# Fewer, wider VectorE operations, squares and row copies on ScalarE, and new tables of places in a hybrid decoder step

## The reference, cut to what matters

```python
for i in range(2):
    mp, ms = modulation(c_prompt, ...), modulation(c_sample, ...)   # six rows of 1024 each
    h = rms_norm(y, norm1_g) * (1 + scale) + shift
    o = mla(h) if i == 0 else sgu_mixer(h)      # attention with a paged cache; gated MLP
    y = y + gate * o
    y = y + gate2 * peer(rms_norm(y, norm2_g) * (1 + scale2) + shift2)

def peer(x):                                    # per token
    q = x @ w_q                                 # 8 heads, two halves of 128
    t1, i1 = top_k(q1 @ keys0.T, 16); t2, i2 = top_k(q2 @ keys1.T, 16)
    top, ci = top_k(t1[:, None] + t2[None, :], 16)          # of 256 candidates
    idx = i1[ci // 16] * 128 + i2[ci % 16]      # 16 of 16384 experts
    act = gelu(dot(u_tab[idx], x))
    return sum(softmax(top) * act * v_tab[idx])
```

## Time and profile before

| | |
|---|---|
| times of three runs | 2204.23, 2215.53, 2223.11 us, median 2215.53 |
| the profiled execution | span 2207.0 us; its own time isn't labelled among the three |
| busy | PE 69%, DVE 63% (1395.3 us), POOL 55%, ACT 16% |
| moved | 751.57 MB, mean 341 GB/s |
| instructions | DVE 3469, ACT 901 |

### The profile page before, as it was taken

The page is one execution under the profiler, slowest core; times in us unless marked ns, Lnnn a source line. Parts: engine busy times, 40 slices in busy tenths (PEclk is TensorE's granted clock), DMA queues, the critical chain, the costliest instruction groups (busy, mean ns, idle before and its releaser), DMA issues. The chain is left out here.

```text
span 2207.0 us, 25764 instructions
## 1 busy us (share of the span) xinstructions
PE 1531.2 (69%) x9198; PEld 745.6 (34%) x9198; DVE 1395.3 (63%) x3469; ACT 355.5 (16%) x901; POOL 1212.1 (55%) x1097
## 2 busy tenths in 40 slices
PE   5676446865546879977687889968778850555567
PEld 2345113541123426533532437525423310111112
DVE  1447988599875655558498836499687327443641
ACT  0100112111112211013131201122223110111111
POOL 0004377545777574437475754467675438745774
PEclk8687778987877979888796888977887785578658
DMA  9719899998989899898798998989998889999998
GB/s 366 276 47 403 291 374 335 413 362 329 384 323 370 297 417 419 341 364 315 274 347 316 315 362 345 377 324 338 363 339 302 323 317 338 380 419 419 335 350 310
DMA packets 213942, 751.57 MB, mean 341 GB/s; under 512 B 27236, under 2 KB 35628, under 8 KB 213816
## 3 DMA queue, kind: packets, MB, share of 16 engines
q0 software_dynamic: 155136, 564.20, 68.4%
q1 hardware_dynamic: 58680, 185.72, 21.6%
HBM read 747.74 MB, written 2.10 MB: 340 GB/s over the span
## 5 line engine op out<-in xcount | busy, mean ns | idle before, releaser
L779 POOL DMA_INDIRECT uring<-in_peer_u,expert x512 | 580.6, 1134 | 511.5 <-DVE dots L1932 211.0
L1217 PE MATMUL yacc<-vring,diag 64*64 64x512 f32 x4096 | 653.6, 738 | 229.9 <-DMA vring<-in_peer_v,expert 163.2
L779 POOL DMA_INDIRECT vring<-in_peer_v,expert x512 | 556.4, 1087 | 425.8 <-PE yacc L1217 290.4
L1932 DVE CUSTOM_DVE_ANT_0 uring<-uring,h 128x1024 f32<-128x1024 f32 x512 | 615.3, 1225 | 161.4 <-DMA uring<-in_peer_u,expert 144.1
L1217 PEld LDWEIGHTS yacc<-vring,diag 64*64 64x64 f32 x4096 | 155.2, 156 | 610.0 <-DMA vring<-in_peer_v,expert 338.8
L1453 ACT ACTIVATE diag<-cst,wts 128x64 f32<-128x64 f32 (+1 forms) x528 | 172.9, 344 | 868.7 <-PE yacc L1217 630.0
L1005 PE MATMUL pp<-hT,wring 128*128 128x128 f32 x992 | 132.3, 294 | 21.7 <-issue 15.9
L1005 PEld LDWEIGHTS pp<-hT,wring 128*128 128x128 f32 x992 | 125.8, 208 | 35.4 <-issue 29.6
L1805 DVE TENSOR_REDUCE arena<-arena 128x16 f32<-128x1024 f32 x64 | 77.8, 1215 | 28.6 <-ACT arena L1392 27.7
L1706 DVE MAX8 t<-sc 128x8 f32<-128x128 f32 (+1 forms) x68 | 19.9, 292 | 117.5 <-ACT sc L1253 83.2
L1068 PE MATMUL pq<-w_uk,arena 128*128 128x512 f32 x128 | 74.6, 672 | 22.9 <-ACT arena L1392 22.9
(11 more groups left out here) (301 smaller groups left out, 1854.0 us busy)
## 6 DMA issues: line engine op xcount, KB each, us to landing
wring<-in_peer_w_q SPq DMA_DIRECT2D x47, 1024.0 KB
wring<-in_w_mod SPq DMA_DIRECT2D x38, 1024.0 KB
wring<-in_sg_w_in SPq DMA_DIRECT2D x48, 768.0 KB
wring<-in_sg_w_out SPq DMA_DIRECT2D x18, 1024.0 KB
wring<-in_mla_w_o SPq DMA_DIRECT2D x9, 1024.0 KB
uring<-in_peer_u,expert POOLq DMA_INDIRECT x512
vring<-in_peer_v,expert POOLq DMA_INDIRECT x512
uring<-in_w_mod SPq DMA_DIRECT2D x6, 1024.0 KB, 16.7
```

Of the source, the lines that this page charges most:

```text
L779: pool.indirect_dma_start(ring[:, slot % RING, :], None, table[n // 3], bass.IndirectOffsetOnAxis(ap=idx, axis=0)).then_inc(land[slot % RI ...
L1217: last = pe.matmul(yacc[64 * q:64 * q + 64, r], diag[at, slot % RING, :], v[at, 512 * q:512 * q + 512], start=first, stop=final)
L1932: dve.tensor_tensor_reduce(u, u, rows_h[:, :], 1.0, 0.0, ALU.mult, ALU.add, dots[:, p % 2, i:i + 1]).then_inc(u_used, 1)
```

## The change

- `rsqrt`: two fused instructions per step in place of four. `polynomial`: two in place of three.
- `pick`: the two sides together, on 512 columns, and one cast of 64 columns for both index pairs. The buffers `cu` and `ti` become one, and `cand` becomes a part of `hot`.
- `norm` of A and B: the sum of squares is an ACT `Square` with an accumulated output into `scr`.
- `gate_row` (in `proj`, `sgu_out` and `peer_out`) and `drain` move to ACT. The label lists follow.
- All five tables are new, with the same units (the sum of squares, the rows and the other stage instructions are places too). In POOL's string the eight K and C stand elsewhere by a few slots: the fourth C, for one, behind 244 U and 212 V before, and behind 249 U and 215 V after. In SP's, one chunk is loaded ahead of `x_prompt`, and 15 chunks ahead of `load_once` where there were 8.

The diff, with the tables' entries left out:

```diff
--- before.py
+++ after.py
@@ -109,67 +109,74 @@
 
 
 PLAN_PE = """
...
 """
 PLAN_ACT = """
...
 """
 PLAN_DVE = """
...
 """
 PLAN_POOL = """
...
 """
 PLAN_SP = """
...
 """
 
 
@@ -282,7 +289,7 @@
         if tile == S:
             rep = ["rep"] if step[3] else []
             return ["ssq", "hT0", "hT1"] + rep, ["sq", "h"], ["hT0", "hT1"] + rep
-        return ["rows", "hT0", "hT1"], ["h"], ["hT0", "hT1"]
+        return ["rows", "hT0", "hT1"], ["h"], ["sq", "hT0", "hT1"]
     if kind == "mla_in":
         return ["z", "cT", "qk"], ["c", "kr", "qk"], ["z", "cT", "qk", "sq"]
     if kind == "attn":
@@ -307,7 +314,7 @@
     if kind == "cache_out":
         return ["oT"], ["oT"], []
     if kind == "proj":
-        return ["row"] * (tile != S) + ["w0", "w1", "w2", "w3"], ["row"] * (tile != S) + ["x"], []
+        return ["row"] * (tile != S) + ["w0", "w1", "w2", "w3"], ["x"], ["row"] * (tile != S)
     if kind == "query":
         return [f"w{i}" for i in range(step[3])] + ["s"], [], ["q", "s"]
     if kind == "route":
@@ -331,9 +338,9 @@
     if kind == "sgu_s_mix":
         return ["ssq", "gT"], ["poly", "sq", "v", "gated", "gT"], ["tanh"]
     if kind == "sgu_out":
-        return ["row"] * (tile != S) + [f"w{i}" for i in range(6)], ["row"] * (tile != S) + ["x"], []
+        return ["row"] * (tile != S) + [f"w{i}" for i in range(6)], ["x"], ["row"] * (tile != S)
     if kind == "peer_out":
-        return ([], ["x"], []) if tile % 3 == S else (["y"], ["x"], [])
+        return ([], ["x"], []) if tile % 3 == S else (["y"], ["x"], ["row"])
     return [], [], []
 
 
@@ -443,9 +450,11 @@
         mrows, mbg = sb("mrows", [P, 12, 256]), sb("mbg", [P, 2, 256])
         scr, rs = sb("scr", [P, 64]), sb("rs", [P, 48])
         sc, work = sb("sc", [P, 4, 2, NKEYS]), sb("work", [P, 256])
-        t1, ti = sb("t1", [P, 2, TOPK]), sb("ti", [P, 2, TOPK], U32)
-        cand, hot = sb("cand", [P, TOPK * TOPK]), sb("hot", [P, TOPK, TOPK])
-        ctop, ci, cu = sb("ctop", [P, TOPK]), sb("ci", [P, TOPK], U32), sb("cu", [P, 2, TOPK], U32)
+        t1, picks = sb("t1", [P, 2, TOPK]), sb("picks", [P, 4, TOPK], U32)
+        cu, ti = picks[:, 0:2, :], picks[:, 2:4, :]
+        hot = sb("hot", [P, 2, TOPK, TOPK])
+        cand = hot[:, 0].rearrange("p a b -> p (a b)")
+        ctop, ci = sb("ctop", [P, TOPK]), sb("ci", [P, TOPK], U32)
         cf, ef = sb("cf", [P, 4, TOPK]), sb("ef", [P, 2, TOPK])
         eg = sb("eg", [P, TOPK + 4])
         kv, kr = sb("kv", [P, 16, KVR]), sb("kr", [P, 2, 16, ROPE])
@@ -586,6 +595,10 @@
         def mod_bank(row):
 
             return yacc[:, row % 2] if row < rows_before(FIRST_QUERY) else pq[:, 1]
+
+        def last_slot(n):
+
+            return SLOT0[max(p for p, s in enumerate(STEPS) if s[0] == n) + 1]
 
         points_seen = {}
 
@@ -1259,6 +1272,10 @@
             def norm(k, tile, layer, second):
                 point(k, 0)
                 begin(act, k)
+                if tile != S:
+                    if k == WHERE[("norm", A, 0, 0)]:
+                        act.wait_ge(in_x, 16)
+                    signal(act.activation(h_tok[tile][:, :], x[tile][:, :], ACT.Square, accum_out=scr[:, 0:1]), "sq")
                 for q in range(2):
                     after(act, PE, k, f"hT{q}")
                     if tile == S:
@@ -1310,6 +1327,23 @@
                         after(act, PE, k, f"pT{f}{q}")
                         signal(copy(att[:, 512 * q:512 * q + 512], ps[q][:, :]), f"pT{f}{q}")
 
+            def gate_row(k, tile, name):
+
+                after(act, PE, k, name)
+                signal(copy(h_tok[tile][:, :], pss[:, :, :].rearrange("p q n -> p (q n)")), "row")
+
+            def projection(k, tile):
+                begin(act, k)
+                if tile != S:
+                    gate_row(k, tile, "row")
+                for j in range(n_points(k) - 1):
+                    point(k, j)
+
+            def peer_out(k, n):
+                if n % 3 != S:
+                    begin(act, k)
+                    gate_row(k, n % 3, "y")
+
             def query(k, n, h, g):
                 begin(act, k)
                 for i in range(g - 1):
@@ -1458,7 +1492,13 @@
                 act.wait_ge(poly_ready, p + 1)
                 act.activation(ew[:, 2, 0:SLOTS[p]], ew[:, 0, 0:SLOTS[p]], ACT.Tanh, scale=GELU_K).then_inc(tanh_ready, 1)
 
-            spot = Spots(PLAN_ACT, D=diagonal, T=tanh)
+            def drain(i):
+
+                n = DRAINED[i]
+                act.wait_ge(v_used, last_slot(n))
+                copy(h_tok[n % 3][:, :], yacc[:, :, :].rearrange("p q n -> p (q n)")).then_inc(drained, 1)
+
+            spot = Spots(PLAN_ACT, D=diagonal, T=tanh, Y=drain)
 
             def point(k, j):
                 early(k, j, ACTE, lambda *a: None)
@@ -1466,7 +1506,7 @@
 
             stages = dict(init=init, norm=norm, mla_in=mla_in, attn=attn, query=query, route=route, query_s=query_s, topk_s=topk_s,
                           cache=cache, sgu_v=sgu_v, sgu_vnorm=sgu_vnorm, sgu_u=sgu_u, sgu_mix=sgu_vnorm,
-                          sgu_s=sgu_s, sgu_s_mix=sgu_s_mix)
+                          sgu_s=sgu_s, sgu_s_mix=sgu_s_mix, proj=projection, sgu_out=projection, peer_out=peer_out)
             for k, s in enumerate(SCHEDULE):
                 signals.start(k)
                 spot()
@@ -1477,7 +1517,7 @@
                         point(k, j)
                 point(k, n_points(k) - 1)
                 signals.end()
-            assert spot.done == dict(D=N_SLOTS, T=len(STEPS))
+            assert spot.done == dict(D=N_SLOTS, T=len(STEPS), Y=len(DRAINED))
 
 
         @block.vector
@@ -1516,9 +1556,8 @@
                 link(ts(out.bitcast(U32), out.bitcast(U32), -1.0, RSQRT_MAGIC, ALU.mult, ALU.add))
                 for _ in range(3):
                     link(tt(tmp, out, out, ALU.mult))
-                    link(tt(tmp, tmp, v, ALU.mult))
-                    link(ts(tmp, tmp, -0.5, 1.5, ALU.mult, ALU.add))
-                    link(tt(out, out, tmp, ALU.mult))
+                    link(stt(tmp, tmp, -0.5, v, ALU.mult, ALU.mult))
+                    link(stt(out, tmp, 1.5, out, ALU.add, ALU.mult))
 
             def square_sum(out, a, waste):
                 link(dve.tensor_tensor_reduce(waste, a, a, 1.0, 0.0, ALU.mult, ALU.add, out))
@@ -1564,7 +1603,7 @@
                 if tile == S:
                     quad_square_sum(k, xr, h)
                 else:
-                    square_sum(scr[:, 0:1], xr, h)
+                    after(dve, ACTE, k, "sq")
                 link(ts(scr[:, 0:1], ps[0][:, 0:1] if tile == S else scr[:, 0:1], 1.0 / D, EPS, ALU.mult, ALU.add))
                 rsqrt(scr[:, 1:2], scr[:, 0:1], rs[:, 0:1])
                 if tile != S:
@@ -1666,20 +1705,12 @@
                 if tile == S:
                     link(tt(h, acc[:, 0, 0:QUAD], sample_rows(mod_row(k))[0], ALU.mult))
                 else:
-                    if SCHEDULE[k][0] == "peer_out":
-                        link(cp(h, flat(pss)))
+                    after(dve, ACTE, k, "row")
                     link(tt(h, h, flat(acc), ALU.mult))
                 signal(tt(x[tile][:, :], x[tile][:, :], h, ALU.add), "x")
 
-            def gate_row(k, tile):
-
-                if tile != S:
-                    after(dve, PE, k, "row")
-                    signal(cp(h_tok[tile][:, :], flat(pss)), "row")
-
             def proj(k, tile):
                 begin(dve, k)
-                gate_row(k, tile)
                 for i in range(4):
                     point(k, i)
                 after(dve, PE, k, "w3")
@@ -1720,13 +1750,12 @@
                 point(k, mid)
                 link(ts(cu[0:r, 0, :], ci[0:r, :], 4, None, ALU.logical_shift_right))
                 link(ts(cu[0:r, 1, :], ci[0:r, :], 15, None, ALU.bitwise_and))
-                link(cp(cf[0:r, 0:2, :], cu[0:r, :, :]))
-                link(cp(cf[0:r, 2:4, :], ti[0:r, :, :]))
-                for i in range(2):
-                    hr = hot[0:r, :, :]
-                    link(tt(hr, over(cf[0:r, i, :], TOPK), times(const("iota16", r), TOPK), ALU.is_equal))
-                    link(tt(hr, hr, times(cf[0:r, 2 + i, :], TOPK), ALU.mult))
-                    link(dve.tensor_reduce(ef[0:r, i, :], hr, X, ALU.add))
+                link(cp(cf[0:r, :, :], picks[0:r, :, :]))
+                hr, h3 = hot[0:r, :, :, :], hot[0:r, :, :, :].rearrange("p i a b -> p (i a) b")
+                link(tt(h3, over(cf[0:r, 0:2, :].rearrange("p i a -> p (i a)"), TOPK), times(const("iota16", r), 2 * TOPK),
+                        ALU.is_equal))
+                link(tt(hr, hr, cf[0:r, 2:4, :].unsqueeze(2).to_broadcast([r, 2, TOPK, TOPK]), ALU.mult))
+                link(dve.tensor_reduce(ef[0:r, :, :].rearrange("p i a -> p (i a)"), h3, X, ALU.add))
                 link(stt(expert_out, ef[0:r, 0, :], float(NKEYS), ef[0:r, 1, :], ALU.mult, ALU.add))
                 after(dve, ACTE, k, "exp")
```

(18 more changed lines are left out.)

113 lines of the change are left out of this document (60 added, 53 removed).

## The result

The changed kernel takes 2240.5 us, median of five runs (2237.4 to 2266.2), against 2212.7 for the kernel before on the same chip. The ratio is 1.0157, with a 95% interval of 1.0103 to 1.0212: slower by one to two per cent, where I forecast 2183 and a range up to 2228. The profiled execution is the slowest of the five (span 2264.4). A second set of runs on another chip gave 1.0218 (1.0156 to 1.0279); its profiled execution is the fastest of its five (span 2223.2).

The account below looks back on a forecast made before the run. The prediction took DMA transfer to bound the kernel, with idle stretches to win back. From 2215.5 us, 4 + 22 + 10 gained and 4 given made 2183.5, say 2183 us, with a range of 2140 to 2228.

Parts of the forecast that it names:

- the DVE-bound stretches: Windows of 10 us with DVE busy 9 or more, transfer partly idle: shorter DVE work was to gain 22 us there.
- my two terms: Gains from less DVE work: 4 us in the serial chain at the start, 22 us where DVE is full.
- the 46 windows: Windows of 10 us with DVE busy 9 or more and DMA share below 0.97, holding 80.6 us of idle transfer.
- DVE's total: Work taken off DVE by picks, roots, polynomials, squares and row copies: about 104 us of its 1395.
- two readings: Gain where DVE is full: 32 us by its share of DVE work, 16 us by POOL's waits for dots; 22 taken.
- the third kind of idleness: Idle transfer where DVE is not full, but PE is or a table's order holds an engine back: 84 us.
- I take -10: New tables: the fourth C later in POOL's table frees eight gathers of 1.24 us from its wait, 10 us gained.
- the bound of +42: Worst case for the new tables: half as much again added to the 84 us of idle transfer where DVE is not full.
- the tables are the larger part: Rival, chance 0.15: a new order also takes half of the 84 us idle where DVE is not full; 2138 us.
- ACT's queue: Rival, chance 0.15: the 20 hand-overs to ACT wait behind diagonals that wait for PE; 2240 us.
- 1.8 us a place: Wait at each of ACT's 20 new places from which nothing is left of the 36 us gained.
- My 4 us: Price given for 20 new waits on ACT (8 squares, 8 gate rows, 4 drains), between 0 and 43 us.

Follow-up runs that it names:

- old_kernel_fourth_c_later: The kernel before with one letter moved, the fourth C of POOL's table ten places later: ratio 1.0026 to the kernel before (0.9991 to 1.0061).

## Why the prediction was wrong

**The bound and the DVE-bound stretches: right.** The first gather came 4 us earlier (POOL's wait for the first gate 161.1 and 156.9 us), as forecast. The idle transfer with DVE full fell by 21 to 23 us, forecast 22. Not all of it need be the shorter instructions' doing: the rewrites alone took away 16 us on one chip, and the tables alone show 44 us there without any rewrite. Alone, under the old tables, the rewrites gave 0.987 and 0.991, 19 to 27 us; my two terms that hold them sum to 26, with the squares and rows in them. (The DVE work in the 46 windows sums to 434 us, not 423, which moves the term by less than 1 us.)

**DVE's total: too large by 30 us.** I had 104 and the trace has 74 of busy time. The step that failed is "each of three steps goes from four instructions to two". The change leaves three: a product and two fused ones. With one saved for two, the 38.5 us for the roots are about 19. The picks, polynomials, squares and copies came out as priced; the remaining 10 us are the gaps of 291 instructions at 0.035, which I had counted in and busy time doesn't hold. The 22 us hardly suffered, for they lay between two readings, which is partly luck.

**The tables: the step that failed.** It is "For the rest, the third kind of idleness, 84 us, bounds it", and of that "I take -10", from the one row in which POOL stood for a C. The run with this letter moved shows 0 (1.0026, 0.9991 to 1.0061). And the tables as a whole cost 3.7%, 77 us on that chip; the bound of +42 was too small by nearly half. I had read which stalls the old order has, and bounded a new order by these. But a new order can make stalls that the old trace doesn't have or has only small: before the bias row PE waited 4.7 us before and 11.9 after, with POOL and DVE standing too, and the gathers fell back by 14 to 16 us across it. My range was also narrower than my own bounds: with +42 in place of -10 the same sum gives 2235.5, and it ended at 2228. The rival that I called "the tables are the larger part" was right in that they are the larger part and wrong in sign, and I gave no chance to the other sign. The parts multiply to somewhat more than the whole (1.037 times 0.987 or 0.991 is 1.024 to 1.028, against 1.016 and 1.022 measured); the difference isn't explained.

**ACT's queue: 2240 us, by another road.** The time is the one that I wrote for this rival, and the mechanism isn't the one; the agreement is chance. The sign I had named, over 1.8 us a place, is met by its letter: 13.0 us for squares and 41.4 for rows are 2.7 us for each of the 20 places. But 34.2 of it is PE's lateness at the very end, which the kernel before has too; without it 1.0 us a place is left. What decides is that with squares and rows taken back 1.0176 remains. My 4 us were too low for the squares if the 0.7 to 0.9% of the two pairs is real, 15 to 20 us; nothing was gained by taking back the rows. Under the old tables the squares do cost 2.1%. There DVE meets ACT late by 45.3 us, 5.7 for each of the eight, so the condition "1.8 us a place" was met there. Probably it is because nothing else was set between the row and the need for its sum, but no run tried that.

**The port rule.** The Trainium skill, SBUF — State Buffer, section "Who interferes with whom", has a DVE instruction with two SBUF inputs and a GpSimd instruction that reads SBUF keep each other off one port, and so spoke against wider picks. The traces agree with the rule, and show its price here to be small. In the kernel before, the 197 gathers that met no instruction of DVE took 0.94 us each, and the 525 that met a dot, which has two inputs in SBUF, 1.25 on average. The gathers that met an elementwise instruction of a pick took 0.98 on average before (62 of them) and 0.99 after (58), so the whole effect of the wider picks is about 1 us. By the same rule the dots, 1.22 us long, hold the port longer than any pick; my "0.43 was the longest" is true of the picks alone.

**What stays open.** That the loss is in the new written order follows from runs: the tables alone, with the old instructions, lose more than the change does. Which part of the order it is stays open. POOL's new order costs 3.9% against the old consumers, and the new consumers lost with every POOL order tried with them, of which the old one is none. The orders of PE, ACT and DVE were not tried one by one either, nor was a new order with the bias row alone loaded sooner. The last gather comes 103 us later with the tables alone than with the rewrites alone, on one chip, and 20 of these arise across the bias row. The rest is spread and not accounted for.

## What to carry to other kernels

When a change brings shorter instructions and a new written order together, forecast the order by itself, and don't bound it by the stalls of the old trace. Look for what is lost by numbering the work and comparing when each number is reached: the longest wait of the new trace (34.8 us) stood where the old one waited 59.3 under another name, and a wait of 11.9 us was where ground was lost. A stall that a trace shows is worth what follows it, which may be nothing. And before shipping, run the new instructions under the old order: here that was all of the gain.

## What the runs showed of the hardware

Chips differ more than this change is worth. The same kernel before took 2212.7, 2187.4 and 2190.2 us in some groups of runs and 2093.0, 2086.9 and 2087.7 in others, at nearly the same granted clock (0.79 and 0.80). Its trace at 2207.0 us moves 341 GB/s; on a faster chip nearly the same kernel (`old_kernel_fourth_c_later`, 2090.1 us) moves 360. Its idle transfer there is 167 us, against 234. The traces of the slower chips also hold only 63 to 68% of the increments by which the gathers' landings are recorded, those of the faster ones over 99%, so counts of increments aren't compared between the two. A forecast in microseconds carries this spread, and a comparison across chips would have hidden or invented any effect studied here.

A gather's issue lengthens beside a dot: 0.94 us when it meets no instruction of DVE, 1.25 on average when it meets a dot (197 and 525 gathers in the trace of the kernel before).
